# Layer one's experts in 12 rounds instead of 16: ranked by tokens on the chip, pairs of 64 seats, weights fetched from loaded addresses

## The reference

```python
def moe(h, router_w, router_b, w1, w3, w2):
    t = h.reshape(-1, D)
    aff = jax.nn.sigmoid(t @ router_w)
    sel = aff + router_b
    ...                                   # best group of 4 experts, then the top 2 in it
    gates = jnp.sum(jax.nn.one_hot(idx, N_EXPERTS) * wsel[..., None], axis=1)
    a = jnp.einsum('nd,edf->nef', t, w1)  # w1, w3: 16 x 1024 x 256
    b = jnp.einsum('nd,edf->nef', t, w3)
    hid = jax.nn.silu(a) * b * gates[..., None]
    return jnp.einsum('nef,efd->nd', hid, w2)   # w2: 16 x 256 x 1024
```

## Time and profile before

| | us |
|---|---|
| median of 3 runs | 1039.26 |
| lowest and highest run | 1034.39, 1042.84 |
| the profiled execution | 1041.76 |
| its span, first to last instruction | 1040.0 |
| TensorE busy in the span | 939.3 (90%) |
| DVE busy | 503.8 (48%) |

### The profile page before, as it was taken

The page is one execution under the profiler, slowest core; times in us unless marked ns, Lnnn a source line. Parts: engine busy times, 40 slices in busy tenths (PEclk is TensorE's granted clock), DMA queues, the critical chain, the costliest instruction groups (busy, mean ns, idle before and its releaser), DMA issues.

```text
span 1040.0 us, 12326 instructions
## 1 busy us (share of the span) xinstructions
PE 939.3 (90%) x4333; PEld 540.8 (52%) x4333; DVE 503.8 (48%) x1169; ACT 255.6 (25%) x618; POOL 186.5 (18%) x221
## 2 busy tenths in 40 slices
PE   2999989989889998999999998999998599699878
PEld 0675545745566446544454447846664464443323
DVE  1216654758887254333333353277477672412124
ACT  2201313535544014110010112031436240301000
POOL 1617120201100001302211101533011100030100
PEclk8999999989989999999999999899999789699989
DMA  9897113568401007568887581922485009859993
GB/s 378 250 288 218 58 40 122 203 243 321 166 1 42 1 1 287 203 236 313 328 331 301 197 298 41 298 100 81 161 284 204 1 1 364 323 198 381 417 405 138
DMA packets 70770, 213.73 MB, mean 206 GB/s; under 512 B 10826, under 2 KB 19298, under 8 KB 61492
## 3 DMA queue, kind: packets, MB, share of 16 engines
q1 hardware_dynamic: 58912, 187.81, 48.3%
q0 software_dynamic: 10624, 21.87, 6.7%
q10 hardware_dynamic: 1172, 3.24, 0.8%
HBM read 201.04 MB, written 23.41 MB: 216 GB/s over the span
## 4 chain that ended last, share of the span: by engine, by line
PE 77%; DVE 11%; issue 4%; DMA 2%; ACT 2%; POOL 2%; SPq 0%; DVEq 0%; ACTq 0%; POOLq 0%
PE bank L1937 16%; PE bank L1847 8%; PE bank L1961 8%; PE bank L1643 8%; PE bank L1539 8%; PE bank L1619 4%; PE bank L1793 4%; PE bank L1631 3%; PE bank L1726 3%; PE bank L1586 3%; DMA BRANCH<-in_w_mod 2%; PE bank L1814 2%; POOL ST L1179 2%; PE bank L1702 2%; PE bank L1912 1%
## 5 line engine op out<-in xcount | busy, mean ns | idle before, releaser
L1937 PE MATMUL bank<-RINGW,NA 128*128 128x512 f32 (+1 forms) x448 | 173.7, 608 | 15.4 <-issue 10.6
L1937 PEld LDWEIGHTS bank<-RINGW,NA 128*128 128x128 f32 (+1 forms) x448 | 68.2, 171 | 113.7 <-issue 113.7
L1179 POOL TENSOR_TENSOR ST<-ST,RT 128x1 f32<-128x1 f32 (+4 forms) x46 | 52.0, 1132 | 415.6 <-DVE ST L2107 228.4
L1643 PE MATMUL bank<-RINGW,H 128*128 128x512 f32 (+4 forms) x384 | 122.4, 480 | 0.0
L1643 PEld LDWEIGHTS bank<-RINGW,H 128*128 128x128 f32 x384 | 71.1, 197 | 49.4 <-issue 44.6
L1847 PE MATMUL bank<-RINGW,H 128*128 128x512 f32 x192 | 84.9, 603 | 0.1
L2667 DVE SCALAR_TENSOR_TENSOR BRANCH<-BRANCH,bank 128x256 f32<-128x256 f32 x24 | 10.1, 421 | 153.9 <-issue 77.7
L1509 ACT ACTIVATE BRANCH<-bank 128x256 f32<-128x256 f32 x24 | 9.2, 385 | 243.2 <-PE bank L1937 243.2
L1243 POOL DMA_INDIRECT pairs<-BRANCH,IDX x21 | 24.1, 1146 | 214.3 <-DVE BRANCH L2691 198.5
L1539 PE MATMUL bank<-IDENT,BRANCH 128*128 128x128 f32 (+1 forms) x311 | 44.8, 292 | 17.3 <-DVE BRANCH L2398 12.2
L1847 PEld LDWEIGHTS bank<-RINGW,H 128*128 128x128 f32 x192 | 36.8, 193 | 45.4 <-issue 45.4
(11 more groups left out here) (328 smaller groups left out, 1521.0 us busy)
## 6 DMA issues: line engine op xcount, KB each, us to landing
RINGW<-in_moe_w SPq DMA_DIRECT2D x56, 1024.0 KB, 10.6
RINGW<-in_w_mod SPq DMA_DIRECT2D x23, 2048.0 KB, 8.1
W2R<-in_moe_w SPq DMA_DIRECT2D x15, 1024.0 KB, 5.1
PROJ<-in_moe_w SPq DMA_DIRECT2D x9, 1024.0 KB, 5.1
RINGW<-in_w_out SPq DMA_DIRECT2D x4, 2048.0 KB, 9.6
WORK<-in_moe_w SPq DMA_DIRECT2D x8, 1024.0 KB, 14.8
RINGW<-in_w_in SPq DMA_DIRECT2D x4, 1536.0 KB, 14.8
pairs<-NA POOLq DMA_DIRECT2D x12, 512.0 KB, 8.3
```

The lines of the kernel that those rows point to most:

```text
L1179: pool.tensor_tensor(r[:, 0:w], m[:, 0:w], POOL_HALF[:, 0:w], ALU.pow).then_inc(rstd_ready, 1)
L1643: ins = pe.matmul(bank_of(s)[:, 0:nn], HT[:, kk, t * P:(t + 1) * P], wv[:, kk, off:off + nn], start=kk == 0, stop=kk == KD - 1)
L1937: ins = pe.matmul(bank_of(s)[seats, :], XGT[n % 2][:, kk, seats], w[:, kk, :], start=kk == 0, stop=kk == KD - 1)
```

## The change

Layer one gets 12 rounds. Experts 0, 1 and 2 keep a round of 128 seats each, by their numbers. Experts 3 to 15 are ranked by their token counts on the chip: the first five in rank (`FULLS`) get a round of 128 seats each, the eight others go in four pairs (`PAIRS`) of 64 seats each, in the order pair, full, pair, full, pair, full, pair, full, full.

- `tot` of layer one, now behind the DVE's copy of xT of round 0, compares every count with every other (13 x 13), makes each expert's rank, and from it `WHO`, the expert number at each of the 13 places. The semaphore `who_ready` tells SP.
- SP loads the 13 experts from addresses that it computes from `WHO` (one register load each, ahead of the expert's DMAs). Layer one's weights may use `WORK` as a fourth slot (every fourth expert), and w2 has five buffers for its first ten experts, then three.
- `slots` reads the table twice, to all partitions and, for the second expert of a pair, to partitions 64 to 127; only the columns of rounds 0 to 2 are made there. `chosen`, a new DVE step behind ab of round 0, picks the other nine columns by products with the ranking's one-hot rows.
- `places`, three small DVE operations, makes the constants for this. `xg` and `gsel` of rounds 3 and up wait for `chosen`.

Layer two's rounds stay as they were.

```diff
+FIXED = 3
+FULLS, PAIRS = 5, 4
+RANKED = N_E - FIXED
+SLOT_STRIDE = (N_E, N_E // 2)
 def rounds(l):
     if l < DEPTH - 1:
-        return [(e,) for e in range(N_E)]
+        out, u = [(e,) for e in range(FIXED)], FIXED
+        for j in range(FULLS):
+            if j < PAIRS:
+                out.append((u, u + 1))
+                u += 2
+            out.append((u,))
+            u += 1
+        return out
     return [(e, e + N_E // 2) for e in range(N_E // 2)]
...
         s += [("h2T", l, t, n) for t in tq if t < 2 for n in (0, 1)]
         early = 0 in sq
+        s += [("places", l)] if early else []
...
-        s += [("pfx", l, 1), ("oh", l, 1), ("gbc2", l), ("tot", l)]
-        s += [("xT", l, 0), ("slots", l), ("xg", l, 1), ("xg", l, 2), ("gdiff", l), ("gsel", l, 0), ("ab", l, 0)]
+        s += [("pfx", l, 1), ("oh", l, 1), ("gbc2", l)]
+        s += [("xT", l, 0), ("tot", l)] if early else [("tot", l), ("xT", l, 0)]
+        s += [("slots", l), ("xg", l, 1), ("xg", l, 2), ("gdiff", l), ("gsel", l, 0), ("ab", l, 0)]
+        s += [("chosen", l)] if early else []
...
+        if p[0] == "w13":
+            j = w13s[p[1]].index(p)
+            if j % 4 < 3 or p == w13s[0][-1]:
+                h = turn_of % SLOTS
+                turn_of += 1
+            else:
+                h = SLOTS
...
-                b = n % 3 if l < DEPTH - 1 else (2, 3, 4, 5, 0, 1, 7, 6)[n % 8]
+                b = (n % 5 if n < 10 else n % 10 % 3) if l < DEPTH - 1 else (2, 3, 4, 5, 0, 1, 7, 6)[n % 8]
...
+                src = a["moe_w2"][l, e] if fixed(l, e) else a["moe_w2"][l][which[0]]
                 sp.dma_start(W2B[b].rearrange("p (k n) -> p k n", k=2),
-                             a["moe_w2"][l, e].rearrange("(k p) n -> p k n", p=P)).then_inc(w2_loaded[b], 16)
+                             src.rearrange("(k p) n -> p k n", p=P)).then_inc(w2_loaded[b], 16)
...
+                    if not fixed(l, e):
+                        if e == FIXED:
+                            sp.wait_ge(who_ready, 1)
+                        c = rank_col(e)
+                        which[0] = sp.value_load(WHO[0:1, c:c + 1], min_val=0, max_val=N_E - 1)
+                    w1 = a["moe_w1"][l, e] if fixed(l, e) else a["moe_w1"][l][which[0]]
+                    w3 = a["moe_w3"][l, e] if fixed(l, e) else a["moe_w3"][l][which[0]]
...
+                    if l < DEPTH - 1:
+                        pool.dma_start(TABE, slots[l].rearrange("(p e) c -> p e c", e=N_E)).then_inc(slots_loaded, 16)
+                        pool.dma_start(TABH[64:P], slots[l][0:64 * N_E, :].rearrange(
+                            "(p e) c -> p e c", e=N_E)).then_inc(slots_loaded, 16)
...
+                        link(dve.scalar_tensor_tensor(key, held, 16.0, RANK, ALU.mult, ALU.add))
+                        ks = key[:, FIXED:N_E]
+                        link(dve.tensor_tensor(AHEAD, ks.unsqueeze(1).broadcast_to([P, RANKED, RANKED]),
+                                               bcast(ks, RANKED), ALU.is_gt))
+                        link(dve.tensor_reduce(rank, AHEAD, AX.X, ALU.add))
+                        link(dve.tensor_tensor(IS_AT, rank.unsqueeze(1).broadcast_to([P, RANKED, RANKED]),
+                                               bcast(PLACE, RANKED), ALU.is_equal))
...
+                        dve.tensor_copy(WHO, WHOF).then_inc(who_ready, 1)
...
+                elif k == "chosen":
...
+                    dve.tensor_tensor(CHOSEN[0:64, 0:PAIRS], among(IS_AT[0:64, 0:PAIRS, :], PAIRS),
+                                      entries(TABE[0:64], PAIRS), ALU.mult)
+                    dve.tensor_tensor(CHOSEN[64:P, 0:PAIRS], among(IS_AT[64:P, PAIRS:2 * PAIRS, :], PAIRS),
+                                      entries(TABH[64:P], PAIRS), ALU.mult)
+                    link(dve.tensor_tensor(CHOSEN[:, PAIRS:PAIRS + FULLS], among(IS_AT[:, 2 * PAIRS:RANKED, :], FULLS),
+                                           entries(TABE, FULLS), ALU.mult))
+                    rest = slice(FIXED, FIXED + PAIRS + FULLS)
+                    link(dve.tensor_reduce(TABS[:, rest, :], CHOSEN, AX.X, ALU.add))
...
+                    dve.tensor_copy(PAIRU[:, rest], TABS[:, rest, 2]).then_inc(index_ready, 1)
```

More of the change, by code:

```diff
@@ L104, in rounds, with seats_of, table_col, rank_col @@
     if l < DEPTH - 1:
-        return [(e,) for e in range(N_E)]
-    return [(e, e + N_E // 2) for e in range(N_E // 2)]
+        out, u = [(e,) for e in range(FIXED)], FIXED
[6 more added lines that the diff above has]
+        return out
+    return [(e, e + N_E // 2) for e in range(N_E // 2)]
+def seats_of(l, r, i):
+    n = P // len(rounds(l)[r])
+    return slice(n * i, n * (i + 1))
+def table_col(l, r):
+    if l == DEPTH - 1 or r < FIXED:
+        return r
+    same = [x for x in range(FIXED, r) if len(rounds(l)[x]) == len(rounds(l)[r])]
+    return FIXED + (PAIRS if len(rounds(l)[r]) == 1 else 0) + len(same)
+def rank_col(u):
+    r = [i for i, us in enumerate(rounds(0)) if u in us][0]
+    c = table_col(0, r) - FIXED
+    return c + (PAIRS if c >= PAIRS else PAIRS * rounds(0)[r].index(u))
 def w2_after(l, e):
@@ L354, in build @@
     home, before, last_in = [], [], {}
-    paired = [p for p in pieces if p[0] == "w13" and len(rounds(p[1])[0]) > 1]
+    w13s = [[p for p in pieces if p[0] == "w13" and p[1] == l] for l in range(DEPTH)]
+    turn_of = 0
     for i, p in enumerate(pieces):
-        if p in paired:
-            i0 = piece_at[paired[0]]
-            h = (i0 % SLOTS, (i0 + 1) % SLOTS, (i0 + 2) % SLOTS, SLOTS)[(i - i0) % 4]
-        else:
-            h = SLOTS + 1 if p == ("modk", 0, MOD_FIRST - 1) else i % SLOTS
+        if p[0] == "w13":
[5 more added lines that the diff above has]
+                h = SLOTS
+        else:
+            h = SLOTS + 1 if p == ("modk", 0, MOD_FIRST - 1) else turn_of % SLOTS
+            turn_of += 1
         home.append(h)
@@ L613, in build @@
         OVER = IDX[:, 2 * T + 2 * N_E:2 * T + 2 * N_E + 1]
+        WHO = IDX[:, 2 * T + 2 * N_E + 1:]
+        WHOF = RT[:, 416:416 + RANKED]
+        TABE = view(M, 9216, N_E, 4)
+        TABH = view(M, 9280, N_E, 4)
+        CHOSEN = view(M, 9344, PAIRS + FULLS, 4, RANKED)
+        AHEAD = view(M, 9344, RANKED, RANKED)
+        PLACE = M[:, 9520:9520 + RANKED]
+        IS_AT = view(M, 9812, RANKED, RANKED)
         assert nc.sbuf_bytes_remaining >= 0
@@ L834, in build @@
                 xg_home[(m, r)] = ((r + 1) % 3, xg_used[(r + 1) % 3])
-        expert_n = lambda l, e: l * N_E + e
-        expert_key = lambda n: (n // N_E, n % N_E)
+        first_round = [sum(len(rounds(m)) for m in range(l)) for l in range(DEPTH)]
+        assert all(n % 2 == 0 for n in first_round)
+        expert_n = lambda l, e: first_round[l] + e
+        expert_key = lambda n: max((l, n - first_round[l]) for l in range(DEPTH) if n >= first_round[l])
+        index_n = lambda l, r: 1 if l == 0 and r < FIXED else l + 2
         resid_at, c = {}, 0
@@ L956, in load_mod, with fixed @@
                              a["w_mod"][p[1]].rearrange("(k p) n -> p k n", p=P)[:, :, c:c + 512]).then_inc(done, 16)
+            which = [None]
+            def fixed(l, u):
+                return l == DEPTH - 1 or u < FIXED
             def load_w2(l, e):
@@ L1037, in _ @@
                     sp.wait_ge(s, v)
-                elif home[i] == SLOTS:
-                    sp.wait_ge(*full_of(("hT", DEPTH - 1, 2, 1, 3)))
+                if home[i] == SLOTS and (not before[i] or before[i][1] < p[1]):
+                    if p[1] == DEPTH - 1:
+                        sp.wait_ge(*full_of(("hT", DEPTH - 1, 2, 1, 3)))
+                    else:
+                        sp.wait_ge(*full_of(("xT", p[1], 0, 1)))
+                        sp.wait_ge(h2_stored, 16 * T)
                 dst, k, l = slot(p), p[0], p[1]
@@ L2629, in _ @@
                 elif k == "oh":
-                    t0, nr = 2 * s[2], len(rounds(l))
+                    t0, nr = 2 * s[2], SLOT_STRIDE[l]
                     seat = lambda r, t, c: SEAT[:, 2 * T * r + 2 * t + c:2 * T * r + 2 * t + c + 1]
```

110 lines of the change are left out of this document (73 added, 37 removed).

## The result

The changed kernel took 1011.47 us (median of 4 runs, 1006.84 to 1012.80) beside 1036.95 us for the kernel before on the same chip (4 runs, 1034.39 to 1042.84): a ratio of 0.9736, 95% interval 0.9701 to 0.9770. It is faster, inside the range of the prediction, but by 25.5 us where 42 were forecast. The profiled execution took 1012.8 us, with a span of 1010.7.

A forecast was written before the change was run, and what follows sets the result against it. It took layer one to be bound by TensorE; -45.6 + 1.2 + 1.3 + 1.0 = -42.1 us takes the profiled 1041.76 to 999.7, the median to 997; own range 993.5 to 1004, 8 in 10 within 988 to 1012.

The forecast's parts named there:

- Four rounds fewer, and pairs: Layer one on TensorE: four whole rounds go, -45.6 us; four rounds become pairs at 11.70 instead of 11.40 us, +1.2.
- The ranking: DVE after round 0's copy: SP's numbers at about 423.5, expert 3's weights asked for at about 424.5, hidden.
- The table read twice: Start of layer one: second read on POOL delays columns and first gather, +1.3 us, between 0 and +4.5.
- Gathers have a queue of their own: Argument against the first gather in layer one waiting for expert 3's weights to drain.
- the dear start: Rival: first gather waits for expert 3's weights and `chosen` loses its cover, about +7 us, 1003; chance 0.08.
- `chosen`, `places`: DVE steps in layer one: `chosen` 2.6 us behind ab of round 0, `places` three operations of 0.2; both hidden, nothing.
- Weights: Layer one's pair at 526.4: 18.4 MB from 480.2 on land just in time or 3.6 us late; +1.0 taken.
- The pairs ahead have 4 to 9 us to spare: Layer one's pairs before the one at 526.4: their weights land 4 to 9 us before they are needed.
- a sign of being wrong: Gaps ahead of the pairs at 480 or 503, or at the first ranked round, would show the forecast wrong.
- transfers bind: Rival: layer one's weights move at 351 GB/s and land 8.2 us late, +9.8 in place of +1.0, 1006; chance 0.16.
- Layer two and the rest: Layer two keeps its code, banks and slots: 0 us.

The follow-up runs named there:

- after_gather: Changed kernel, but SP asks for expert 3's weights only when the gather of round 1 has landed: 1001.43 us, ratio to before 0.9658.
- w13_first: As all three edits, but expert 3's w1 and w3 go out at once; its w2 and all behind it wait for round 1's gather: 994.27 us.
- one_earlier: As w13_first, but each expert's w2 is asked for one place later from expert 7 in rank on instead of 8: 993.11 us.
- table_split: Changed kernel, with a semaphore of its own for the second table read; `slots` waits for the first read only, `chosen` for the second: 1003.29 us.
- fixed_addresses: Changed kernel, with constants in place of register loads for the 13 experts' addresses, the wait for the ranking kept: 1010.15 us.
- all three edits: Changed kernel with the edits of after_gather, table_split and w2_later together: 1001.32 us, ratio to before 0.9654.
- after_table: Changed kernel, but SP asks for expert 3's weights when both table reads have landed, without waiting for the gather: 1008.53 us.
- w2_later: Changed kernel, but from expert 8 in rank on each w2 is asked for behind the next expert's w1 and w3: 1004.62 us.
- lean_w2: Changed kernel, loading only the first eighth of w2 for the experts at places 9, 10 and 11, order and waits kept: 1002.04 us.

## Why the prediction was right in its sign and off by 15 us

- **Four rounds fewer, and pairs:** right. R changed by -36.7 us, which is -45.6 + 1.2 and 7.4 of waits for weights (0.69 + 0.22 + 3.68 + 2.78), to 0.3 us. A pair costs what was forecast: its ab, the transposes and the y between them are 6.87 + 1.24 + 3.44 = 11.55 us, and the single round behind it 6.87 + 1.09 + 3.58 = 11.54, together 0.29 over two rounds of 11.40, where 0.30 stood.
- **The ranking:** right. SP's numbers were ready at 424.63, its first load went out at 425.68, where 423.5 and 424.5 stood; 1.5 us of the difference are scatter of the start.
- **The table read twice: the step that failed.** It said "+1.3 us on the path, between 0 and +4.5", and it was +11.0: 2.9 us of the read, 5.15 of the gather, 2.3 of the lower clock behind the idle time, and 0.7 that stay without the weights. With the weights out of the way it is 0.7 (after_gather), and 0.2 with the reads apart, so the cost of the second read itself was right. What failed is "Its landing took 4.6 us": that was the landing of a gather on an empty DMA. The same row gives 9.2 as the median and 12.1 as the most, which are the later gathers, with weights beside them; the change puts weights beside the first as well, and so its row was the 9.2. The bound of +4.5 let 3 MB drain from 425 on; it forgot that the read too would wait (2.9 us), which brings the gather to 431.96, just when expert 4's 3 MB are asked for, and that TensorE would then run at the lower clock (2.3 us).
- **"Gathers have a queue of their own"**, the argument against the dear start, does not protect them. In the runs the first gather lands in 4.6 us alone (after_gather), in 5.0 behind 2 MB asked for 3.6 us earlier (w13_first), in 6.5 behind 2 MB asked for 2.7 us earlier (one_earlier), in 7.7 behind 3 MB asked for 2.9 us earlier (table_split), in 8.6 behind 3 MB asked for 2.4 us earlier (fixed_addresses), and in 9.0 to 9.7 with 3 MB asked for within 0.6 us of its issue. The Trainium skill, "DMA: Bandwidth & Descriptors", section Queues, rings and completion order, says that each of the 16 DMA engines takes its queues in turn, packet by packet; these landings agree with that, and with it in view the rival should have had more than 0.08. Only half of that rival came: it let the first gather wait for the weights, but the cover of `chosen`, which it saw lost, held.
- **`chosen`, `places`:** right, nothing. `chosen` ended at 437.6, when TensorE waited for the gather until 441.7; in after_gather ab of round 1 starts at 435.62, where y of round 0 ends (432.18 + 3.44), so it is hidden there too.
- **Weights:** the place was right (experts 12 and 13), the size wrong: +1.0, bounds to +3.6, where 7.4 us were measured. Between the time at which SP gets past w2 of expert 8, 492.9, and the landing at 543.6, the changed kernel's queues moved (packets, MB, share of 16 engines):

```profile
q1 hardware_dynamic: 3052, 16.96, 82.5%
q0 software_dynamic: 1241, 3.08, 15.4%
```

  20.0 MB instead of 18.4: 1.2 MB more of weights, most likely of loads still under way when the count begins or asked for before it ends (expert 13's w2 at 539.97, expert 14's w1 at 541.13), and 0.4 more of gathers and scatters. They moved at 395 GB/s instead of 417, because the DMA was at its full speed only in the middle: 363 GB/s at a share of 0.97 from 492.9 to 500, 418 at 1.02 from 500 to 537, and 308 at 0.79 from 537 to 543.6. In that last stretch SP held the next load until 539.97, so part of the DMA engines' time stood empty while the pair still waited for its bytes; a sum of bytes at one speed has no such end. And the term left out the slower ab behind the gap, 2.78 us, though the rival had it. "The pairs ahead have 4 to 9 us to spare" was wrong too: experts 9 and 10 waited 0.69 us, at the pair forecast for 503, where a gap was named as a sign of being wrong.
- **The rival "transfers bind"** had the mechanism and nearly the price (+9.8 for 7.4), not the reason: in the stretches shown with a share over 1 the queue moved 411 to 421 GB/s, not 351. The figure of about 358 GB/s from the Trainium skill, "DMA: Bandwidth & Descriptors", section Where 436 GB/s comes from, which the prediction set beside this rival, was not the limit in these runs: the kernel with all three edits moved 412 to 421 GB/s for 85 us.
- **Layer two and the rest:** no effect; the 5.1 us there are a lower clock in the profiled execution of before. (The sentence that TensorE's row of slices falls below 9 only between stages was too strong: its last slices, 8, 7 and 8, lie in layer two's rounds, where the gaps of the earlier trace rows are. The forecast doesn't rest on it.)
- **The chances:** the two rivals were given as alternatives to each other, with 0.16 and 0.08, but nothing keeps both from coming, and both came: 997 + 9.7 + 6.4 = 1013, against 1011.5 measured. The forecast's own range, 993.5 to 1004, missed the time. The range of 988 to 1012 was drawn to reach either rival alone; that both together still ended inside it, by half a microsecond, is luck.

What stays open: why the clock of TensorE in layer two was lower in the profiled execution of before, and what share of before's other executions was like it; only that one was traced.

## What to carry to other kernels

When a change asks for bytes earlier, price what they will lie beside: each small transfer on the path takes the landing time of its kind with the queues full, not the one it had on an empty DMA, and a wait of two transfers in a row counts twice. The remedy is an order by need: let the megabytes that can wait stand behind the kilobytes that TensorE waits for, but no longer than that, since a stage at the limit of its bytes pays for an empty queue at its far end (2 MB asked for 8.4 us sooner gave 6.4 us here). Two rivals that do not exclude each other should be added up as a case of their own.

## What the runs showed of the hardware

- A read of 16 KB landed in 1.9 to 2.0 us on a quiet DMA (after_gather, after_table), in 4.7 to 5.2 us when 3 MB of weights were asked for at the same time on another queue (the changed kernel, table_split, w2_later, lean_w2), and in 6.4 when they had been asked for 0.9 us earlier (fixed_addresses).
- With all three edits, single rounds of 3 MB and pairs of 6 MB of weights kept the DMA full at 412 to 421 GB/s for 85 us, gathers and scatters among them.
- In the changed kernel TensorE ran at the lower clock level after 3.68 us of idling (granted clock 0.50), and a pair's ab took 9.65 us; after 0.69 us it stayed at the higher (1.00), with 7.09.
- Addresses loaded into a register cost the 39 loads nothing that S, R or the time shows (fixed_addresses).
